# Two-layer encoder trunk on one core: second-layer query and key norms in groups of four, gate input before the last queries, score masks together

## The reference

```python
h = rmsnorm(x, mix_norm[1])
c_u, c_v, cq, ckv, kr = split(h @ o_w_in)          # 512, 512, 384, 256, 32
yc = gelu(c_u) * (mask(w_s) . rmsnorm(gelu(c_v)) + bias)
q  = rmsnorm(cq) @ w_uq                            # 8 heads x (64 plain + 32 rotary)
kv = rmsnorm(ckv) @ w_ukv                          # 8 heads x (64 key + 64 value)
q_nope, q_rope = rmsnorm per head, rope on q_rope
k_nope = rmsnorm per head; k_rope = rope(rmsnorm(kr)), shared by all heads
sc = q . k, set to -1e30 where a key's 64-frame chunk is after the query's
yd = softmax(sc) @ v
x = x + concat(rmsnorm(yc), rmsnorm(yd)) @ o_w_out
```

## Time and profile before

| What | us |
|---|---|
| median of three timed runs | 1135.97 (1135.8 to 1135.98) |
| the profiled execution | 1136.32 |
| its span, first to last instruction | 1134.4 |
| PE busy | 1123.2 |
| DVE busy | 570.4 |
| ACT busy | 437.4 |
| POOL busy | 106.4 |

### The profile page before, as it was taken

How to read it: one execution, slowest core, us unless ns; L and a number is a source line. 1 busy time by engine, 2 the same in 40 slices (tenths; PEclk the granted TensorE clock), 3 DMA queues, 4 the chain that set the end, 5 groups by cost and what they waited for, 6 DMA issues and landing times.

```text
span 1134.4 us, 13645 instructions
## 1 busy us (share of the span) xinstructions
PE 1123.2 (99%) x5075; PEld 899.5 (79%) x5075; DVE 570.4 (50%) x787; ACT 437.4 (39%) x682; POOL 106.4 (9%) x146
## 2 busy tenths in 40 slices
PE   8999999999999999999999999999999999999998
PEld 7777678888888888888877774688888888888887
DVE  6678877434434433242565788666433443441321
ACT  5545445323223322131446667644322322332210
POOL 6000000001001000000202211000100100100000
PEclk9999999999999999999999999999999999999999
DMA  6512223323333322322332210122332333322231
GB/s 192 195 56 75 75 64 103 112 93 93 95 106 95 92 93 99 105 94 79 85 94 81 76 37 2 56 93 93 93 111 92 92 94 105 98 91 95 84 124 52
DMA packets 83961, 103.90 MB, mean 92 GB/s; under 512 B 9547, under 2 KB 60432, under 8 KB 83792
## 3 DMA queue, kind: packets, MB, share of 16 engines
q1 hardware_dynamic: 82848, 103.04, 29.2%
q0 software_dynamic: 1056, 0.30, 0.1%
q10 hardware_dynamic: 16, 0.00, 0.0%
HBM read 101.23 MB, written 2.10 MB: 91 GB/s over the span
## 4 chain that ended last, share of the span: by engine, by line
PE 94%; DVE 5%; ACT 1%; issue 1%; ACTq 0%; DVEq 0%
PE ps L1635 29%; PE ps L1637 29%; PE ps L1636 29%; PE ps L1668 2%; PE ps L2023 1%; PE ps L2051 1%; DVE e_pT L1253 1%; DVE o_p L1521 0%; PE ps L2038 0%; DVE w_lo L1084 0%; DVE tiny L1512 0%; PE ps L1756 0%; PE ps L1688 0%; DVE e_sc L1245 0%; DVE acc L1258 0%
## 5 line engine op out<-in xcount | busy, mean ns | idle before, releaser
L1084 DVE TENSOR_TENSOR w_lo<-raw,w_hi 128x1024 fp32r<-128x1024 f32 (+2 forms) x194 | 227.8, 1181 | 425.9 <-ACT w_hi L675 423.1
L675 ACT ACTIVATE w_hi<-raw 128x1024 fp32r<-128x1024 f32 (+2 forms) x194 | 195.7, 1016 | 463.3 <-PE ps L1637 446.1
L1635 PE MATMUL ps<-h_hi,w_hi 128*128 128x512 f32 x928 | 367.3, 396 | 2.2 <-DVE w_lo L1084 1.1
L1637 PE MATMUL ps<-h_hi,w_lo 128*128 128x512 f32 x928 | 361.4, 389 | 0.0
L1636 PE MATMUL ps<-h_lo,w_hi 128*128 128x512 f32 x928 | 361.3, 389 | 0.0
L1635 PEld LDWEIGHTS ps<-h_hi,w_hi 128*128 128x128 f32 x928 | 174.2, 188 | 43.4 <-issue 6.1
L1636 PEld LDWEIGHTS ps<-h_lo,w_hi 128*128 128x128 f32 x928 | 174.3, 188 | 38.3 <-issue 2.6
L1637 PEld LDWEIGHTS ps<-h_hi,w_lo 128*128 128x128 f32 x928 | 174.2, 188 | 36.5
L566 POOL TENSOR_TENSOR ffn_t<-ffn_t,row_scale 128x512 f32<-128x512 f32 x40 | 50.9, 1294 | 641.1 <-ACT ffn_t L853 641.1
L1635 PE MATMUL ps<-w_hi,act_hi 128*128 128x512 f32 x176 | 68.6, 390 | 0.0
L1637 PE MATMUL ps<-w_hi,act_lo 128*128 128x512 f32 x176 | 68.5, 389 | 0.0
(11 more groups left out here) (276 smaller groups left out, 1214.5 us busy)
## 6 DMA issues: line engine op xcount, KB each, us to landing
raw<-in_w_ffn_in SPq DMA_DIRECT2D x88, 512.0 KB, 3.5
raw<-in_w_ffn_out SPq DMA_DIRECT2D x44, 512.0 KB, 3.7
raw<-in_e_w_in SPq DMA_DIRECT2D x18, 512.0 KB, 3.7
raw<-in_o_w_in SPq DMA_DIRECT2D x8, 512.0 KB, 3.6
raw<-in_o_w_out SPq DMA_DIRECT2D x8, 512.0 KB, 3.5
x_tok<-in_x SPq DMA_DIRECT2D x4, 512.0 KB, 4.0
raw<-in_e_w_out SPq DMA_DIRECT2D x8, 256.0 KB, 3.8
raw<-in_e_w_out SPq DMA_DIRECT2D x4, 512.0 KB, 4.0
```

Of the source, the lines that this page charges most:

```text
L675: ins = act.activation(dst, src, ACT.Copy)
L1084: ins = TT(dst, src, high, ALU.subtract)
L1635: MM(dst, st_hi, mv_hi, start=start, stop=False)
L1637: return MM(dst, st_lo, mv_hi, start=False, stop=stop)
```

## The change

**Norms by four.** Squares of four tiles are summed by four products with 32 weight columns each (`sums4`), that write the partition strips 0, 32, 64 and 96 of one bank; one norm (`rms`) works on that bank; four products with 32 rows of weights (`spread`), with a selection matrix `sel`, carry the strips to four banks, 128 partitions each. There are 3 norms (two for queries, one for keys) in place of 12. DVE multiplies the spread result by the tile (`q_scale`, `k_norm`), POOL no longer does. ACT multiplies the keys by their gain (`key_gains`) in place of DVE.

**Order.** PE: `q_load(0)`, `q_load(1)`, `cu_load(0)`, sums, `cu_load(1)`, spread, `cu_load(2)`, `cu_load(3)`, `q_load(2)`, gate products, `q_load(3)`, `key_tiles(0)`, sums, `key_tiles(1)`, spread, key sums, `value_tiles(0)`, spread, the mean M_OC, `value_tiles(1)`, scores. The gMLP branch is done up to its norm ahead of the attention loop; scaling and split stay in it. The tiles `yc`, `u_c` and `k_sq` lie elsewhere.

**Masks.** The four score tiles stand together, then three mask products (one of 256 columns). **First layer.** PE makes `sel` with four strip products and ACT copies it; two pairs of semaphores become one each.

```diff
-O_UQ, O_CU = (104, 105, 108, 109), (106, 107, 110, 111)
+O_UQ, O_CU = (104, 105, 110, 111), (106, 107, 108, 109)
...
-    V_BANKS = ((0, 1), (3, 4))
+    V_BANKS = ((0, 2), (3, 2))
+    MASKS = ((0, slice(384, 512)), (1, slice(256, 512)), (2, slice(128, 256)))
+    MASKED_BY = (1, 2, 2, 3)
...
@@ gpsimd
-        for h in range(HEADS):
-            m = M_OQ + h
-            pool.wait_ge(rs_ready, m + 1)
-            pool.tensor_tensor(o_q[:, h, :], o_q[:, h, :], rs[:, m % 2, :], ALU.mult).then_inc(rs_used, 1)
...
@@ scalar
+        act.activation(sel[:, :], ps[:, 7, 128:256], ACT.Copy, scale=4.0).then_inc(gains_ready, 1)
...
         q_squares(0, 4)
+        through(104)
         q_squares(1, 6)
         through(105)
-        rms(M_OQ, ps[:, 4, :], 1)
...
+        through(106)
+        rms(M_OQ, ps[:, 4, :], 1)
...
+        q_squares(2, 4)
+        through(110)
+        rms_table()
+        q_squares(3, 6)
+        yc_square(0)
+        yc_square(1)
         key_squares(0)
+        rms(M_OQ + 1, ps[:, 3, :], 1)
+        key_gains(0)
         key_squares(1)
+        key_gains(1)
+        rms(M_OK, ps[:, 4, :], 1)
+        yc_square(2)
+        yc_square(3)
+        value_copy(0)
+        rms(M_OC, ps[:, 1, :], 512)
+        exp_table()
+        value_copy(1)
         through(111)
...
@@ vector
+        def q_scale(r, banks):
+            dve.wait_ge(rs_spread, r + 1)
+            dve.sem_inc(rs_used, 1)
+            for g, b in enumerate(banks):
+                h = 4 * r + g
+                TT(o_q[:, h, :], ps[:, b, :], o_q[:, h, :], ALU.mult).then_inc(oq_scaled, 1)
...
+            for a, h in ((0, 2 * p), (64, 2 * p + 1)):
+                TT(o_k[a:a + 64, h, :], ps[a:a + 64, 4 + p, :], k_pairs[p // 2][a:a + 64, p % 2, :], ALU.mult
+                   ).then_inc(ok_normed, 1)
...
+        yc_gate(0)
+        yc_gate(1)
+        q_tiles(3, 6)
+        yc_gate(2)
+        yc_gate(3)
+        rms(M_OQ + 1, ps[:, 3, :], 1)
+        yc_sum(1)
+        q_scale(1, (0, 1, 2, 3))
+        rms(M_OK, ps[:, 4, :], 1)
+        yc_sum(2)
+        yc_sum(3)
+        value_copy(0)
+        k_norm(0)
+        rms(M_OC, ps[:, 1, :], 512)
+        value_copy(1)
+        k_norm(1)
...
         o_max(0)
+        through(111)
+        k_norm(2)
         o_prob(0)
         o_max(1)
+        k_norm(3)
         o_pt(0)
         o_prob(1)
         o_max(2)
+        yc_norm(0)
         o_pt(1)
...
@@ tensor
+        def sums4(bank, weights, tiles):
+            for g in range(4):
+                ins = MM(ps[32 * g:32 * g + 32, bank, :], weights[g], tiles[g], start=True, stop=True)
+            ins.then_inc(sums_ready, 1)
+
+        def spread(m, banks):
+            pe.wait_ge(rs_ready, m + 1)
+            for g, b in enumerate(banks):
+                ins = MM(ps[:, b, :], sel[32 * g:32 * g + 32, :], rs_of(m)[32 * g:32 * g + 32, :], start=True, stop=True)
+            ins.then_inc(rs_spread, 1)
...
+        for g in range(4):
+            MM(ps[32 * g:32 * g + 32, 7, 128:256], ident[:, 48:80], mean64, start=True, stop=True)
...
-        cu_load(0, lambda: q_means(0, 4))
-        q_means(1, 6)
+        cu_load(0)
+        q_sums(0, 4)
         cu_load(1)
+        spread(M_OQ, (4, 5, 6, 7))
+        cu_load(2)
+        cu_load(3)
+        pe.wait_ge(oq_scaled, 2)
         q_load(2, 4)
...
+        key_tiles(0)
+        pe.wait_ge(gates_ready, 4)
+        q_sums(1, 3)
+        key_tiles(1)
+        spread(M_OQ + 1, (0, 1, 2, 3))
+        pe.wait_ge(ok_squared, 4)
+        pe.wait_ge(ok_gained, 1)
+        sums4(4, [mean64[:, 48:80]] * 4, [k_sq[:, p, :] for p in range(4)])
         value_tiles(0)
+        pe.wait_ge(ok_gained, 4)
+        spread(M_OK, (4, 5, 6, 7))
+        pe.wait_ge(oq_scaled, 6)
+        pe.wait_ge(yc_summed, 4)
+        mean(M_OC, 1, ones, acc[:, :])
         value_tiles(1)
...
-                MM(s_, o_q[:, h, i * P:(i + 1) * P], o_k[:, h, 0:P * (i + 1)], start=True, stop=False)
-
-                MM(s_[:, P * i:P * (i + 1)], mask_q[:, :], mask_k[:, :], start=False, stop=True
+                MM(score(i), o_q[:, h, i * P:(i + 1) * P], o_k[:, h, 0:P * (i + 1)], start=i != 0, stop=False)
+            for bank, c in MASKS:
+                MM(ps[:, bank, c], mask_q[:, :], mask_k[:, 0:c.stop - c.start], start=False, stop=True
                    ).then_inc(d_scores, 1)
```

More of the change, by code:

```diff
@@ L521, in _ @@
         pool.memset(mask_q[:, 64:128], 0.0)
[L522 to L523 removed]
+        for c in (0, P):
+            pool.memset(mask_k[:, c:c + 64], 0.0)
+            ins = pool.memset(mask_k[:, c + 64:c + 128], NEG)
+        ins.then_inc(columns_set, 1)
         n_gain = [0]
@@ L938, in q_squares, with gelu_table, key_squares, key_gains @@
                 act.activation(q_sq(h), ps[:, b0 + i, :], ACT.Square).then_inc(oq_squared, 1)
+        def gelu_table():
+            act.activation(spare[:, :], eps_col[:, :], ACT.Gelu_apprx_tanh)
+        def key_squares(half):
+            act.wait_ge(keys_done, half + 1)
+            for j in range(2):
+                act.activation(k_sq[:, 2 * half + j, :], ps[:, 4 + 2 * half + j, :], ACT.Square).then_inc(ok_squared, 1)
+        def key_gains(half):
+            for j in range(2):
+                act.wait_ge(ok_squared, 2 * half + j + 1)
+                act.activation(k_pairs[half][:, j, :], ps[:, 4 + 2 * half + j, :], ACT.Copy, scale=g_col(G_OK)
+                               ).then_inc(ok_gained, 1)
+        def value_copy(half):
+            act.wait_ge(load_used, O_UKV + half + 1)
+            act.activation(o_v[:, 0:2, 256 * half:256 * half + 256],
+                           ps[:, V_BANKS[half][0], :].rearrange("p (t c) -> p t c", t=2), ACT.Copy).then_inc(ov_act, 1)
+        def yc_square(j):
+            act.wait_ge(yc_ready, j + 1)
+            if j >= 2:
+                act.wait_ge(yc_summed, j - 1)
+            act.activation(yc_sq[:, j % 2, :], yc[:, j, :], ACT.Square).then_inc(yc_squared, 1)
         q_squares(0, 4)
+        through(104)
         q_squares(1, 6)
         through(105)
-        rms(M_OQ, ps[:, 4, :], 1)
[L944 to L948, removed]
         act.wait_ge(kr_rotated, 1)
@@ L961, in _ @@
                        ).then_inc(cv_square, 1)
-        q_squares(2, 4)
-        q_squares(3, 6)
+        through(107)
+        gelu_table()
         through(109)
[L965 to L969, removed]
         for j in range(4):
@@ L1604, in _ @@
         dve.sem_inc(rs_used, 1)
+        o_pt(4)
+        yc_low(1)
+        o_prob(5)
+        o_max(6)
         yc_low(2)
+        o_pt(5)
+        yd_sum(1)
+        o_prob(6)
+        o_max(7)
+        o_pt(6)
         yc_low(3)
+        o_prob(7)
         o_pt(7)
@@ L1961, in _ @@
         pe.wait_ge(cv_ready, 4)
-        cu_load(0, lambda: q_means(0, 4))
-        q_means(1, 6)
+        cu_load(0)
+        q_sums(0, 4)
         cu_load(1)
-        pe.wait_ge(rs_step, M_OQ + 2)
+        spread(M_OQ, (4, 5, 6, 7))
+        cu_load(2)
+        cu_load(3)
+        pe.wait_ge(oq_scaled, 2)
         q_load(2, 4)
-        pe.wait_ge(rs_step, M_OQ + 4)
+        pe.wait_ge(u_scaled, 4)
+        pe.wait_ge(cv_normed, 4)
+        for g0 in range(0, 8, 2):
+            for t, g in ((t, g) for t in range(QT) for g in (g0, g0 + 1)):
+                a = 64 * (g % 2)
+                ins = MM(ps[a:a + 64, g // 2, t * P:(t + 1) * P], v_c[:, t, 64 * g:64 * g + 64], w_spT[:, g, :],
+                         start=True, stop=True)
+        ins.then_inc(gates_mixed, 1)
+        pe.wait_ge(oq_scaled, 4)
         q_load(3, 6)
-        cu_load(2, lambda: q_means(2, 4))
-        q_means(3, 6)
-        cu_load(3)
         def key_tiles(half):
```

259 lines of the change are left out of this document (79 added, 180 removed).

## The result

The changed kernel took 1130.06 us, the median of five runs (1129.18 to 1130.68), for 1135.98 before: ratio 0.9947, 95% interval 0.9936 to 0.9957. That is 5.9 us faster, where 8.5 was forecast; it lies inside the range (1124.5 to 1133.0) and on the forecast side. The profiled execution took 1130.68 us with a span of 1128.8, for 1136.32 and 1134.4 before.

A forecast was written before the change was run, and what follows sets the result against it. TensorE (PE) work or PE waits were taken to bound the kernel; -2.6 (stretch one), -6.2 (the loop) and +0.4 (Layer one) sum to -8.4, from 1136.3 to 1127.9 profiled, 1127.5 as median; range 1124.5 to 1133.0 us.

The forecast's parts named there:

- stretch one: First query load to first attention scores, 63.61 us before: only less PE work helps; forecast -2.6 us.
- the loop: First attention scores to first output load, 47.54 us before: forecast 41.3 us, laid out head by head, so -6.2.
- the ring: In the attention loop: next head's scores reuse the previous head's banks and wait for its exponentials; 4.2 us a turn.
- the group at 1.0 us: Before the scores: each of six groups of four sum or spread products costs 1.0 us, 6.0 in all.
- A: Sum and spread groups: quarters overlap only in pairs, six groups cost +5.0 us, ending at 1132.5; chance 0.14.
- B: Sum and spread groups: quarters don't overlap, +14 us, ending at 1141.7, slower than before; chance 0.07.
- Rival D: Norms before the scores: a chain comes late, each of three spreads waits 1 us more, 1130.5; chance 0.07.
- Layer one: First layer: four strip products and the change of form on PE cost +0.4 us, bounds 0.2 to 1.1.
- The term between 0.05 and 0.33: Attention scores: cost in us of each of the second and third masks of a head, taken as 0.16.
- C: Attention loop: DVE binds it, the loop takes 43.5 us, +2.2, ending at 1129.7; chance 0.12.
- E: Whole change: the ring swallows the mask saving and waits the rest, 1136 within 0.2%; chance 0.04.
- sign of being wrong: Three: a spread waits over 1 us for rs_ready, the loop exceeds 44 us, the end moves less than first output load.

The follow-up runs named there:

- experiment 6: Changed kernel with each of the three groups of four spread products made twice: 1132.10 us.
- experiment 3: Changed kernel with DVE's split of load 115 moved from before the first scaling of probabilities to behind yc_norm(1): 1128.58 us.
- experiment 10: Kernel of experiment 7 with DVE's split of load 115 moved from behind the fifth maxima to behind the last ones: 1127.84 us.
- experiment 4: Changed kernel with two unread 128x512 products, one each behind the scores of heads 0 and 1: 1129.75 us.
- experiment 1: Kernel before the change with the grouped masks alone (four score tiles, then three masks): 1136.66 us, ratio 1.0008.
- experiment 2: Changed kernel with a mask after each score tile again: 1132.77 us.
- experiment 8: Kernel of experiment 7 with head 0's first mask right behind its tile and k_norm(1) behind the first maxima: 1130.96 us.
- experiment 5: Changed kernel with the gMLP norm (M_OC mean, table loads, yc copies and norms) put back into the attention loop: 1131.87 us.
- experiment 7: Kernel of experiment 3 with k_norm(3) behind the third maxima, yc_norm(0) and yc's split one head later, load split behind the fifth maxima: 1128.49 us.
- experiment 9: Kernel of experiment 8 plus the two unread 128x512 products of experiment 4: 1129.93 us.

## Why the prediction was right, and where it was off

**The bound.** Right. In stretch one only PE work counts (experiment 6: 2.6 us more of it cost 2.4). In the loop it is PE and the ring through DVE and ACT in turn: five of its eight steps have PE's own length (6.10, 6.10, 6.11) or the ring's (4.17, 4.23), as laid out.

**Stretch one, -1.67 for -2.6.** The step that failed is the group at 1.0 us, "0.86 plus about 0.15 for leaving and entering the strip form". It measured 1.13 to 1.28. Six times some 0.2 is 1.3 us, which is how far PE's work there is off (-2.1 for -3.4). I had read full overlap out of the rows of halves rightly, and rightly refused A and B; but the earlier trace rows show many products in one form, over which one entry and one exit are spread, and each group of four pays both alone. The estimate of 1.12 us a group, from the Trainium skill (TensorE: Matmul & The Clock Gate, Measured speedup vs the span model), stood nearer: the adjacent group at 1.13 agrees with it, the lone ones are above. The waits came out shorter than planned, 0.44 us in all (61.94 less 61.50) for 0.8, and so hid a part of that: the M_OC mean waits 0.38 (forecast 0.2), while the second spread waits some 0.1 at most, by the 0.43 from the product ahead of it for 0.32 at the first, and the third about as much (forecast 0.4 and 0.2). Rival D, a chain late by 1 us per spread, is refuted. That POOL's products became DVE's cost nothing: DVE is busy 39.10 of 61.94 us.

**Layer one, +0.51 for +0.4.** The same surcharge, once.

**Masks.** The term between 0.05 and 0.33 for the second and third mask was taken at 0.16. Measured, a head's scores and masks last 692.35 to 694.93, 2.58 us; less 2.15 for the tiles and 0.33 for the first mask, 0.05 is left for each of the others: the lower bound. PE was busy 36.8 us in the loop at full clock (experiments 3 and 10), where I had 37.4. This made the PE steps 6.1 for the 6.2 and 6.3 planned.

**The loop, -4.56 for -6.2.** The 1.7 us between the 41.3 planned and 42.98 lie in three places. The third step took 5.96 for 5.0: there the clock fell (at full clock, in experiment 4, the step takes 5.21, so 0.75 of it is the clock), which I had given a chance of 0.01 with the words that no row hints at it. The rows of before indeed show none, but my own layout did foresee PE idle in the first two steps, and I didn't ask what that would do to the clock. The second step took 5.81 for 5.4: I had seen the split and k_norm(2) in front, and had priced them 0.4 short. The ring's own steps took 4.17, 4.23 and 4.50 for 4.0, 4.0 and 4.2, together 0.7 more. The PE steps gave 0.4 back.

**The rivals.** C gave 1129.7 and D 1130.5, nearer to the result than my 1127.5, and yet neither is what happened. C named the right engine, but DVE's amount of work does not bind the loop: in experiment 10 it does the same 37.6 us of work in 40.23. What bound was DVE's order, the places of the load split and of k_norm(3). E is refuted for the whole change, but it is what the masks do when alone (experiment 1).

**The range and the signs.** The low end, 1124.5, was said to be 3 us of cheaper masks and absent waits; those two terms give 0.9 (four steps of 0.22) and 0.8, so 1.7. One sign of being wrong did show, by a hair: the end moved 5.6 us and the first output load 5.7. The other two did not: no spread waited 1 us, and the loop is under 44.

**Left open.** Why the clock falls in some runs of one kernel and not in others, and what in experiment 1 delays it until 685.63, no run settles. The idle stretches alone don't decide it: experiment 6's profiled execution has those of the changed kernel to 0.01 us and no fall. What the norms by four bring without the new order was not run either; experiment 2 shows both together. The wait of 1.52 before the second scores, a turn of the ring with three masks together, was only filled or traded (experiments 4 and 8), never shortened with all masks together; with a mask after each tile it is 0.41 (experiment 2).

## What to carry to other kernels

Two savings may need each other: cutting PE's work in the loop by some 7 us (45.08 to 38.2) brought nothing while DVE and ACT set the pace, and 2.7 once their norms were out of the loop; so ask of every cut which engine the stage then waits for, and test each part with and without the other. When an engine goes from full to waiting, read the queue of the engine that it waits for, for work that isn't due yet: one load split of 1.2 us, moved within DVE's order, was worth 1.5 us here, and 2.2 once a key norm had moved too and the split stood in a later idle stretch of DVE. Price a short group in another tile form by its own entry and exit, never from a long run of products in that form.

## What the runs showed of the hardware

Four fp32 products in strips of 32 (rows or columns) over 512 columns run at once: 0.86 us per group in a row of like groups, 1.13 where one form follows another, and 1.20 to 1.28 alone between full products. That is 2.7 to 3.0 times as fast as four full ones (3.44); the Trainium skill (TensorE: Matmul & The Clock Gate, Measured speedup vs the span model) has 3.07 for four row strips, which the group behind another one reaches and the lone ones don't.

A mask product of one row costs 0.33 us between fp32 tiles, but two further ones directly behind it, one of them of 256 columns, about 0.05 each (2.58 us for a head's scores and masks, less 2.15 for the tiles and 0.33).

The clock of an all but saturated PE fell to its 1.2 GHz level behind short idle stretches: 1.52 and 1.55 us in the changed kernel (two runs of five; scores of 2.40 took 4.06) and in experiments 5 and 6, which share them (two of five and one of five), 0.79 and 1.75 in experiment 8 (five of five), 1.52, 0.66 and 1.17 in experiment 1 (nine of eleven), and there once more behind 1.77. No run shows a mean clock under 1.000 with 1.52 and 0.42 (experiments 3, 7 and 10, fifteen runs), with 0.41 and 0.68 (experiment 2, six) or with the stretches filled (experiments 4 and 9, ten). So such stretches went with the fall, but the same ones brought it in five runs of fifteen only. Two unread products are a cheap guard where such waits can't be avoided; to take the wait away was better.
